# Stick-breaking heads summed by parts: a running sum of the weights against differences of neighbouring values

## What is computed

```python
z = jnp.einsum('bqhd,bkhd->bhqk', qb, kb).astype(jnp.float32) * scale
mask = jnp.arange(end)[None, :] < (start + jnp.arange(Q_BLOCK))[:, None]
log_1mb = jnp.where(mask, jax.nn.log_sigmoid(-z), 0.0)
suffix = lax.cumsum(log_1mb, axis=3, reverse=True) - log_1mb
a = jnp.where(mask, jnp.exp(jax.nn.log_sigmoid(z) + suffix), 0.0)
outs.append(jnp.einsum('bhqk,bkhd->bqhd', a.astype(vb.dtype), vb))
```

## Time and profile before

| | us |
|---|---|
| median of 3 runs (3780.5 to 3785.68) | 3780.61 |
| the profiled execution, its own time | 3782.12 |
| its span, first to last instruction | 3780.4 |
| stick steps, first half, 765 to 843 | 78 |
| stick steps, second half, 2507 to 2716 | 209 |

### The profile page before, as it was taken

One profiled execution on the slowest core, in us unless ns is written; L12 is line 12 of the kernel. 1 busy time (PEld: TensorE's weight loads), 2 busy tenths in 40 slices (PEclk: granted clock), 3 DMA queues, 4 the chain that ended last, 5 costly groups with the idle time before them and its releaser, 6 DMA issues.

```text
span 3780.4 us, 52091 instructions
## 1 busy us (share of the span) xinstructions
PE 3527.1 (93%) x22042; PEld 2940.5 (78%) x22042; DVE 2197.6 (58%) x2777; ACT 1203.5 (32%) x1983; POOL 1887.2 (50%) x1306
## 2 busy tenths in 40 slices
PE   7989999978999999999899999978899999999998
PEld 6878877857778787887778888766688787878877
DVE  7754576377364545456764466547777446454545
ACT  2122112267222222223122122346666322222223
POOL 4232433579355555546333323737688436555455
PEclk9999999999999999999999999989999999999999
DMA  3100412534201111114111132351122201111111
GB/s 121 35 27 31 150 52 80 181 112 129 89 23 45 56 45 56 64 38 151 35 34 40 33 147 73 123 178 45 45 84 80 78 32 42 45 56 56 45 67 62
DMA packets 79050, 272.68 MB, mean 72 GB/s; under 512 B 8929, under 2 KB 9185, under 8 KB 76514
## 3 DMA queue, kind: packets, MB, share of 16 engines
q1 hardware_dynamic: 70176, 239.11, 18.7%
q10 hardware_dynamic: 8642, 30.24, 2.1%
HBM read 221.08 MB, written 48.23 MB: 71 GB/s over the span
## 4 chain that ended last, share of the span: by engine, by line
PE 69%; DVE 17%; POOL 6%; ACT 4%; issue 3%; DMA 0%; POOLq 0%; SPq 0%; DVEq 0%; ACTq 0%
PE ps L1403 19%; PE ps L1404 19%; PE ps L1405 19%; PE ps L1409 3%; DVE acc L2096 3%; PE ps L1703 2%; POOL rowa L2680 2%; DVE tf_lo_p L2095 2%; PE ps L1673 2%; DVE rowb L2620 1%; PE ps L1674 1%; DVE af_hi_p L2095 1%; POOL rowc L2680 1%; ACT wd_hi L1754 1%; DVE af_lo_p L2095 1%
## 5 line engine op out<-in xcount | busy, mean ns | idle before, releaser
L2680 POOL TENSOR_TENSOR ring_lo<-ring_raw,ring_hi 128x512 fp32r<-128x512 f32 (+1 forms) x356 | 599.9, 1691 | 381.7 <-ACT ring_hi L1754 371.9
L1403 PE MATMUL ps<-a_hi,ring_hi 128*128 128x512 f32 x1472 | 590.0, 401 | 27.8 <-DVE af_hi_p L2095 14.7
L1404 PE MATMUL ps<-a_lo,ring_hi 128*128 128x512 f32 x1472 | 577.1, 392 | 0.0
L1405 PE MATMUL ps<-a_hi,ring_lo 128*128 128x512 f32 x1472 | 576.9, 392 | 0.0
L1403 PEld LDWEIGHTS ps<-a_hi,ring_hi 128*128 128x128 f32 x1472 | 278.5, 189 | 102.3 <-DVE af_hi_p L2095 22.3
L1405 PEld LDWEIGHTS ps<-a_hi,ring_lo 128*128 128x128 f32 x1472 | 278.5, 189 | 60.1
L2095 DVE TENSOR_TENSOR xres<-xres,ps 128x512 f32<-128x512 f32 x352 | 234.8, 683 | 148.8 <-PE ps L1405 146.4
L1404 PEld LDWEIGHTS ps<-a_lo,ring_hi 128*128 128x128 f32 x1472 | 278.9, 189 | 54.3
L2680 POOL TENSOR_TENSOR rowa<-rowa,rowb 128x1152 f32<-128x1152 f32 (+11 forms) x64 | 255.0, 3993 | 104.3 <-DVE rowb L2620 101.6
L1403 PE MATMUL ps<-wd_hi,af_hi 128*128 128x512 f32 x704 | 277.8, 395 | 23.4 <-DVE xres L2095 17.6
L2681 POOL TENSOR_SCALAR ring_hi<-ring_raw 128x1024 fp32r<-128x1024 f32 x78 | 101.6, 1302 | 365.9 <-PE ps L1405 319.3
(11 more groups left out here) (305 smaller groups left out, 8267.3 us busy)
## 6 DMA issues: line engine op xcount, KB each, us to landing
ring_raw<-w SPq DMA_DIRECT2D x92, 512.0 KB, 3.5
ring_raw<-wgu SPq DMA_DIRECT2D x68, 512.0 KB, 3.6
uq<-q_scr SPq DMA_DIRECT2D x96, 256.0 KB, 4.6
ring_raw<-wd SPq DMA_DIRECT2D x34, 512.0 KB, 3.6
ring_raw<-wo SPq DMA_DIRECT2D x32, 512.0 KB, 3.9
uk<-k_scr SPq DMA_DIRECT2D x6, 2048.0 KB, 10.6
rlf<-wgu SPq DMA_DIRECT2D x20, 512.0 KB, 4.4
xraw<-xt SPq DMA_DIRECT2D x16, 512.0 KB, 7.3
```

The costliest lines, as they stand in the source:

```text
L1403: pe.matmul(o, ah, bh, start=begin and i == 0, stop=False)
L1404: pe.matmul(o, ah, bl, start=False, stop=False)
L1405: last = pe.matmul(o, al, bh, start=False, stop=end and i == len(pairs) - 1)
L2680: tt = lambda o, a, b, op: pool.tensor_tensor(o, a, b, op=op)
```

## The change

Let W[s] be the sum of A[j] over j >= s. Then W[s] = (1 - beta[s]) W[s+1] + beta[s], and the sum of A[s] v[s] equals the sum of W[s] (v[s] - v[s-1]), with v[-1] = 0.

- The scan takes both rows, multiplies by `rb` and adds `ra`, and writes W into `ra`. POOL's product is gone; PE's transposes wait for "scan" instead of "attn", and an `rb` row is free when its scan is done.
- A buffer `uv_shifted` (UVS) takes the values one key position earlier by two transfers, `load_before`, right behind `load_v` of the two s units: rows 0 to 126 of the scratch tensor into partitions 1 to 127, and row 127 of every tile into partition 0 of the next tile. POOL zeroes the first place and subtracts UVS from `uv` in place (`differences`, emitted in iterations 0 and 6).
- UVS lies on the third `rb` row, so the s steps use two `rb` rows instead of three in the second half, three instead of four in the first.

```diff
@@ plan_attention
+                if what == "v" and UNITS[u][0] == "s":
+                    emit("load_before", hf, u, [("shifted", hf, u - 1)] if u else env["free"])
...
+        singles = (0, 1) if hf else (0, 1, 3)
...
+                    z = singles[x % len(singles)] if unit[0] == "s" else x % NR
...
         def stick(st):
             emit("stick", hf, st)
-            row_free[1][st["x"] % NR] = [("attn", hf, st["x"])]
+            row_free[1][st["z"]] = [("scan", hf, st["x"])]
...
+                for u in range(2):
+                    if st and x == 6 * u:
+                        while ("v", u) not in loaded:
+                            yield False
+                        emit("differences", hf, u)
@@ tensor
-                    for mark in new("pe", [("attn", hf, st["x"])]):
+                    for mark in new("pe", [("scan" if st["kind"] == "s" else "attn", hf, st["x"])]):
...
-                        for mark in new("pe", [(f"ld_v{u % 2}", hf, u)]):
+                        for mark in new("pe", [("shifted", hf, u) if st["kind"] == "s" else (f"ld_v{u % 2}", hf, u)]):
@@ vector
-                g = st["rb"][:, 0:128 * st["n"]][:, ::-1]
+                beta, g = (row[:, 0:128 * st["n"]][:, ::-1] for row in (st["ra"], st["rb"]))
...
-                dve.tensor_tensor_scan(g, g, g, 1.0, op0=ALU.mult, op1=ALU.bypass).then_inc(*up("scan", hf, st["x"]))
+                dve.tensor_tensor_scan(beta, g, beta, 0.0, op0=ALU.mult, op1=ALU.add).then_inc(*up("scan", hf, st["x"]))
@@ gpsimd
-            elif kind == "stick":
...
-                tt(st["ra"][:, 0:L - 1], st["ra"][:, 0:L - 1], st["rb"][:, 1:L], ALU.mult).then_inc(*up("attn", hf, st["x"]))
+            elif kind == "differences":
...
+                    pool.memset(UVS[0:1, 0, :], 0.0).then_inc(*up("first_zero", hf))
...
+                tt(UV[u][:, 0:nt, :], UV[u][:, 0:nt, :], UVS[:, 0:nt, :], ALU.subtract).then_inc(*up("shifted", hf, u))
@@ sync
+            elif kind == "load_before":
...
+                sp.dma_start(UVS[1:128, 0:nt, :], vsc[u, 0:127, 0:nt, :]).then_inc(*up("ld_before", hf, u, 0, by=16))
+                sp.dma_start(UVS[0:1, 1:nt, :], vsc[u, 127:128, 0:nt - 1, :]).then_inc(*up("ld_before", hf, u, 1, by=16))
```

More of the change, by code:

```diff
@@ L62 @@
     ("pool_pool", "pool_head pool_hist"),
-    ("pool_attn", "weight weighted attn o_var o_rs o_normed"),
+    ("pool_attn", "weight weighted first_zero shifted attn o_var o_rs o_normed"),
     ("act_out", "out_sq out_scaled"),
@@ L266, in build @@
               [sb(f"rowd{i}", [1024], W0 + 32768 + 4096 * i) for i in range(4)])
+    UVS = sb("uv_shifted", [16, 128], W0 + 40960)
     ORAW = [sb(f"oraw{i}", [8, 128], R0 + 8192 + 4096 * i) for i in range(2)]
@@ L1048, in plan_attention @@
         LV = NA - 1
-        row_free = [[[] for _ in range(NA)], [[] for _ in range(NR)]]
+        row_free = [[[] for _ in range(NA)], [[] for _ in range(2)] + [[("shifted", hf, 1)]] + [[] for _ in range(3, NR)]]
+        singles = (0, 1) if hf else (0, 1, 3)
         steps = []
@@ L1054, in plan_attention @@
                     x = len(steps)
+                    z = singles[x % len(singles)] if unit[0] == "s" else x % NR
                     steps.append(dict(u=u, kind=unit[0], mt=int(unit[1]) + (2 if unit[0] == "d" else 6), i=i, hh=hh,
                                       n=8 * hf + i + 1, x=x, last=i % 4 == 3 and (unit[0] == "d" or hh == 1),
-                                      ra=rows_a[x % NA], rb=rows_b[x % NR], p=x % 12))
+                                      ra=rows_a[x % NA], rb=rows_b[z], z=z, p=x % 12))
         cnt = {"s": 0, "t": 0, "b": 0, "o": 0}
@@ L1069, in scores @@
             free = list(dict.fromkeys(m for z in range(nb) for m in grab(BK[j + z])))
-            emit("scores", hf, st, r, b, j, width, free, row_free[0][st["x"] % NA], row_free[1][st["x"] % NR],
+            emit("scores", hf, st, r, b, j, width, free, row_free[0][st["x"] % NA], row_free[1][st["z"]],
                  stat.get(st["x"] - 12, []) if b == 0 else [])
@@ L1092, in combine @@
             emit("combine", hf, st)
-            row_free[1][st["x"] % NR] = [("attn", hf, st["x"])]
+            row_free[1][st["z"]] = [("attn", hf, st["x"])]
         def stick(st):
             emit("stick", hf, st)
-            row_free[1][st["x"] % NR] = [("attn", hf, st["x"])]
+            row_free[1][st["z"]] = [("scan", hf, st["x"])]
         def tbank():
@@ L1747, in quarter, with env_free @@
         return (a[:, lo_], b[:, hi_], a[:, hi_], a[:, lo_], b[:, lo_], b[:, hi_], a[:, hi_])[k]
+    def env_free(hf):
+        return [("wino_c", hf, PAIRS2[-1], 1, 0)]
     def env_start(hf, which):
@@ L2880, in gpsimd @@
                 tt(ra, ra, rb, ALU.add).then_inc(*up("attn", hf, st["x"]))
-            elif kind == "stick":
-                hf, st = a
-                L = 128 * st["n"]
-                for mark in new("pool", [("scan", hf, st["x"])]):
+            elif kind == "differences":
+                hf, u = a
+                nt = 8 * hf + 8
+                if u == 0:
+                    for mark in new("pool", env_free(hf)):
+                        pool.wait_ge(*at(*mark))
+                    pool.memset(UVS[0:1, 0, :], 0.0).then_inc(*up("first_zero", hf))
+                    for mark in new("pool", [("first_zero", hf)]):
+                        pool.wait_ge(*at(*mark))
+                for mark in new("pool", [(f"ld_v{u % 2}", hf, u), ("ld_before", hf, u, 0), ("ld_before", hf, u, 1)]):
                     pool.wait_ge(*at(*mark))
-                tt(st["ra"][:, 0:L - 1], st["ra"][:, 0:L - 1], st["rb"][:, 1:L], ALU.mult).then_inc(*up("attn", hf, st["x"]))
+                tt(UV[u][:, 0:nt, :], UV[u][:, 0:nt, :], UVS[:, 0:nt, :], ALU.subtract).then_inc(*up("shifted", hf, u))
             elif kind == "o_norm":
@@ L2952, in sync @@
                     sp.dma_start(UV[u % 2][:, 0:nt, :], vsc[u, :, 0:nt, :]).then_inc(*up(f"ld_v{u % 2}", hf, u, by=16))
+            elif kind == "load_before":
+                hf, u, held = a
+                nt = 8 * hf + 8
+                for mark in new("sp", held):
+                    sp.wait_ge(*at(*mark))
+                sp.dma_start(UVS[1:128, 0:nt, :], vsc[u, 0:127, 0:nt, :]).then_inc(*up("ld_before", hf, u, 0, by=16))
+                sp.dma_start(UVS[0:1, 1:nt, :], vsc[u, 127:128, 0:nt - 1, :]).then_inc(*up("ld_before", hf, u, 1, by=16))
             elif kind == "load_q":
```

## The result

| | before | after |
|---|---|---|
| median of the runs beside each other, us | 3783.14 | 3803.86 (3798.17 to 3806.69) |
| ratio, 95% interval | | 1.0048 (1.0035 to 1.006) |
| the profiled execution and its span, us | 3782.12, 3780.4 | 3806.69, 3804.9 |

A forecast was written before the change was run, and what follows sets the result against it. VectorE's scan and POOL's product, excluding each other, were taken to bound the stick stages in both halves. Gains of 30 + 3 + 7 less 1.5 gave 38.5 us, from 3780.6 to 3742 us; range 3718 to 3768.

The forecast's parts named there:

- Term (6): Added transfers on SP, large and small: nothing due behind them, landing in time; cost 0, up to 2 us.
- Term (1): Second-half stick steps: POOL's products leave the sum locked with VectorE's scans; gain 30 us, bounds 18 to 44.
- term (3): First softmax step behind the second-half stick stage: VectorE's minimum comes sooner after the last scan; gain 3 us, 0 to 5.
- rival A: Stick steps: PE and ScalarE hold each other, only POOL's waits go; gain 17 us, 3764 us; chance 0.18.
- Rival C: Stick steps: new scan costs up to 4.34 ns a column, 43 us slower, 3824; chance 0.06, including a scan dear by half.
- Rival D: Stick steps: the lock isn't what it seems, waits pass to ScalarE; gain below 7 us, 3777 us; chance 0.04.
- Term (4): First-half stick steps: POOL's norm product and the copies come less late; gain 7 us, 2 to 12.
- Term (5): Four added subtractions on POOL, two in each half, priced like products, mostly in idle time; cost 1.5 us, 0 to 5.8.
- Term (7): One row fewer for beta's complement in each half, free when its scan ends; cost 0, cover 1.2 us a step.
- (2): Fill ahead of the second-half stick steps, 2507 to 2519.9: waits for ScalarE, not POOL; gain 0.

The follow-up runs named there:

- f1_split: The changed kernel with its 127-partition transfer of the shifted values cut into 112 and 15 partitions: 3754.7 us, ratio 0.9927; repeated, 3751.8 us.
- n_half2: f1_split with the first transpose group of head-1 stick steps copied by VectorE instead of ScalarE, in the second half only: 3736.8 us, ratio 0.9881.
- k_before_copies: The kernel before with the first transpose group of every stick step copied by VectorE, for head 1 too, in both halves: 3789.1 us, ratio 1.0012.
- h_no_product: The kernel before without POOL's product, so PE transposes plain betas and an `rb` row is free with its scan: 3757.2 us, ratio 0.9932.
- i_rows: The kernel before with only the change's row plan, two `rb` rows in the second half, three in the first, freed by POOL's product: 3831.0 us, ratio 1.0124.

## Why the prediction was wrong, point by point

- **Term (6), the added transfers, is the step that failed.** It priced "four transfers of 508 KB and 1016 KB and four small ones" by their issue (0.47 to 0.59 us) and by the landing of a like load (5.6 us), 0 and up to 2 us. The like load has 128 partitions, the added one 127. It ran on one DMA engine at 26 GB/s, and cost 33 us ahead of the second half (1695.1 against 1662.1 us in f1_split; 29.6 of them are ScalarE's wait for the spill), 12 in the stage of the first (85.0 against 72.9) and 5 ahead of it (766.1 against 761.0); from f1_split to after the medians differ by 49 us. The term also named what stands behind the added transfers in SP's queue and found none of it due, but left out the spill of the values, for which the first sigmoid waits; "up to 2" was its price for a late spill. The sentence on what would show the term wrong, the first sigmoid coming later after the last projection, was the right place to look (34.4 us instead of 4.8). The Trainium skill has the rule, "DMA: Bandwidth & Descriptors", section "Why a DMA increments its semaphore by 16 and not by 1": a transfer takes the largest number of engines up to 16 that divides the slowest dimension of both its sides, with 127 partitions as its example for a single engine; the trace agrees with its share of 0.06. It speaks directly against this change, and the prediction didn't weigh it.
- **Term (1), 30 us: the mechanism was right, the size was off.** Taken alone, the rest of the change shortened the second-half stage from 210.3 to 189.1 us, 21 us, of which the seam of term (3) is a part. The scans came out as forecast: 3.35 us for 1536 columns, none at 4.4. PE's busy time was worked out as 150 us and measured as 146.8. What was mis-sized is the rest for ScalarE's copies: 10 taken, 20.8 measured (20.3 in after), so rival A's mechanism was the real one, and the prediction's own sign against the term, more than 15 us of such waits, came true; PE was busy 87% of that stage in after (147.0 of 168.7 us), where above 90% was forecast. The guess "leave 10" had no row behind it; the order of ScalarE's queue in a head-1 step would have given it, a pair of microsecond sigmoids ahead of two copies. With that order mended (n_half2) 9.4 us of waits are left, and the stage lasts 153.5 us where 160 was forecast.
- **Rival C** is refuted. A scan with an addition and two different rows costs the same: 3353 ns for 1536 columns is 2.18 ns a column, against 2.17 for the old one. What the prediction cited from the Trainium skill, "DVE: opcode table, instruction layouts, handler registers and perf-mode slots", section "Datapath and trigger behaviour", has the scan program run at half throughput, with no word of its operations; the trace agrees in that the new pair of operations costs what the old one did.
- **Rival D** is refuted by k_before_copies and h_no_product together: the product did hold the stage, and while it was there, relief for ScalarE brought nothing.
- **Term (4), 7 us for the first half:** 5.1 measured in f1_split. POOL's norm product is waited for as long as before, 5.3 against 5.8 us, so the guess that it came late through the stick products was wrong; the copies are what shrank.
- **Term (5), 1.5 us for the subtractions:** within what can be told. The subtractions cost more than the products' price: 4.5 to 5.2 us for 2048 columns where 3.9 was taken, 2.3 to 3.0 for 1024 where 1.9 was. In f1_split one scan of 1408 columns is held by the second one, which runs until 2520.9: two scans take 7.9 us there from 2519.0, and 6.2 later. So the new scan and POOL exclude each other as the old one did.
- **Term (7), 0 for the spare row:** right, by f1_split (0.7 us of waits for a row). The cover held; i_rows shows what the same row plan costs where the product frees the row, 45 us.
- **Terms (2) and (3)** are small and not measured apart. In f1_split PE waits 1.4 us for VectorE's minimum behind the last scan, where it was 3.7.

With the transfers cut, the time is 3754.7 and 3751.8 us in two groups of runs, inside the range of 3718 to 3768 and 10 to 13 us above the forecast, nearly all of it term (1).

## What to carry to other kernels

A load "like" one in the trace is only like it if its partition count is: price an added transfer by how many DMA engines it can be cut over, and cut a shifted load of 127 partitions into 112 and 15 before anything else (in f1_split the subtraction of the second unit then begins 19 us after the first piece is issued, early enough here). A slow transfer is paid for by whoever needs the DMA engines next, here a spill some thirty microseconds on, so look at what is due behind it on any queue. And when a bound is lifted, read the queue of the next engine in its order, not its busy share: ScalarE was at 78% and still made PE wait nineteen times.

## What the runs showed of the hardware that was not expected

- 1016 KB to 127 partitions, issued by SP, move at 26 GB/s with a DMA share of 0.06; issued by ScalarE they are slow too (up to 68.6 us, beside SP's transfers); issued by POOL they land in 8.3 us. The Trainium skill, "DMA: Bandwidth & Descriptors", in the section on the increment by 16, has this too, as an exception for some transfers from GpSimd; the run agrees.
- A slow transfer holds back transfers of another engine's queue: 38.6 us for a spill that takes 4.3. The Trainium skill, "DMA: Bandwidth & Descriptors", section "Issuing engines are not separate DMA queues", says that all of them end on the same 16 engines and interleave. The trace agrees with both: beside SP's transfers the slow one moved at some 15 GB/s, and alone at 26. Interleaving didn't help the spill, which landed when the slow transfer did; that it stood behind the pieces of SP's earlier transfers is the likely reason and isn't shown.
- Behind such a transfer an issuing engine isn't stopped at once: SP passes the transfer itself in 0.29 us and stands on the next one, for 24.5 and 27.2 us, whether that is 7.5 KB or a load of weights. How much it may have in flight before it stops was not measured.
